# Reordering the first stages of a two-layer streaming encoder: where the norms, the weight splits and the sums of squares stand

## The chip, the cores and the metric

The kernel runs on one core of one Trainium2 chip. The metric is the device time of one execution in microseconds (us), the median of three runs. Engines are named as the profile names them: PE is TensorE (PEld its weight loads), DVE VectorE, ACT ScalarE, POOL GpSimd, SP the engine that issues the weight transfers.

## What is computed

One step of a two-layer encoder in float32 for 1024 prompt frames and 32 sample frames of 1024 channels. Cut to what matters:

```python
# layer 0: convolution module, then SwiGLU
h = rms_norm(x, g_mix0); u = h @ w_pw1 + b_pw1          # 1024 -> 2048
g = a * sigmoid(gate)                                    # a, gate = halves of u
c = depthwise_conv(g, w_dw, width 31, causal) + b_dw     # per channel
x = x + silu(layer_norm(c)) @ w_pw2 + b_pw2
x = x + (silu(rms_norm(x) @ w_gate) * (rms_norm(x) @ w_up)) @ w_down
# layer 1: sliding-window attention with per-head norms, then SwiGLU
q, k, v = split(rms_norm(x) @ w_qkv); x = x + attention(q, k, v) @ w_o
x = x + swiglu(rms_norm(x))
```

## The kernel before

The frames are held transposed (channels on the partitions) in two halves: A is frames 0 to 511 (one PSUM bank per tile), B is frames 512 to 1055 (two banks of 272 columns). Each float32 product is made of three faster products: activations and weights are split in a high part (`hAh`, `whi`) and a rest (`hAl`, `wlo`), and a tile is high x high, rest x high and high x rest. ACT writes the high part of each weight block (`hi()`, line 857), POOL the rest (`lo()`, line 1909), SP loads the raw block. `proj` (lines 346 and 355) is one tile: for each of 8 channel blocks k it waits for `h_ready` (both parts of the activations), multiplies both with `whi`, runs a piece of other PE work (`mid`), and then multiplies the high part with `wlo`. An A tile has 24 products of 512 columns, a B tile 48 of 272.

The order of the program is written out by hand for every engine, and each engine runs its list in order. The list `SEQ1` is the first stage, the tiles of `w_pw1`: gate tiles `g` and value tiles `a` of half A for the first three channel blocks, then A and B in turns, and at its end B's tiles of blocks 0 and 1. `SEQ1` index 0 to 28 is called tile 0 to 28 below. Ahead of it lie 18 groups of transposes of x (`x_group`, line 401), eight of them before tile 0, and the products `xn` that transpose and norm half A at once (line 427: x times a diagonal of the frames' norm factors, `diag`).

- While `SEQ1` runs, DVE turns each pair of tiles into a GLU output (`glu`, lines 1469 and 1475) and does the depthwise convolution of half A (`conv`, lines 1504 to 1520) in two PSUM banks X and Y, 4 and 5; ACT makes 10 of the 31 taps' products (`taps`, line 987), and POOL adds them (line 1940). After each channel block POOL adds it to a sum over channels (`csum`, line 1962).
- When `conv` of A is done, PE makes the layer norm's mean from `csum` (line 364), DVE centres (1534), ACT squares, PE sums the eight squares in float32 (`square_mean`, line 381), ACT makes the factor (`factor`, lines 881 to 885), DVE multiplies (1542), ACT does SiLU (902) and the high part (906), DVE the rest (1406), in two buffers `nrm` that are used in turns (`sq` in the profile). Only then do the eight tiles `p2` of half A run, followed by B's last tiles, half A's next norm `ffn0A`, and the feed-forward tiles.
- PSUM: banks 0 to 3 are a ring from which `take` gives the tiles their banks, 4 to 7 a second ring (transposes, head norms) or the convolution's. A bank is handed out again when its reader has released it.
- Norms later in the program (`norm_parts`): DVE x_norm (1401), ACT high part (893), DVE rest (1406), two channel blocks at a time. Their mean (`norm_mean`) takes banks of the first ring, in the middle of a tile.

## Time and profile before

| | before |
|---|---|
| median of 3 runs | 2289.23 us (2288.8 to 2289.9) |
| the profiled execution, its own time | 2286.99 us |
| its span, first to last instruction | 2285.2 us |
| mean granted PE clock | 0.988 |
| PE busy | 2228.7 us, 98% |
| POOL, DVE, ACT busy | 1113.6, 1111.8, 1037.8 us |

The profiled execution is 2.2 us below the median; 1.8 us of it lie outside the span. PE's idle time inside the span is 2285.2 less 2228.7, 56.5 us.

### The profile page before, as it was taken

What the parts mean: (1) busy time and instruction counts of PE and PEld (TensorE: products, weight loads), DVE (VectorE), ACT (ScalarE), POOL (GpSimd) and SP (SyncE); (2) the same over time, 40 slices, a digit from 0 to 9 for tenths busy, and PEclk for the clock granted to TensorE, in tenths of its full rate; (3) what the DMA queues carried; (4) which work ended last, traced back from release to release, by engine and by line L of the source; (5) the groups of instructions that cost most, each with busy time, mean ns of one, the idle gap of its engine ahead of it and who ended that gap; (6) DMA issues with size and microseconds to landing.
All of it is one profiled execution on the core that took longest, in us unless ns stands there. A gap on an engine that the chain in (4) does not pass through costs nothing.

```text
span 2285.2 us, 34556 instructions
## 1 busy us (share of the span) xinstructions
PE 2228.7 (98%) x13954; PEld 2017.0 (88%) x13954; DVE 1111.8 (49%) x1822; ACT 1037.8 (45%) x1659; POOL 1113.6 (49%) x573
## 2 busy tenths in 40 slices
PE   8998899999999999999999999999999999999999
PEld 7797678887889799999999898888888989999999
DVE  4987668873434544445443535454554142222223
ACT  6544655533524654544552466465655332222222
POOL 3787569975446533333334544333333443443433
PEclk9999899999999999999999999999999999999999
DMA  4111123332333522222222342222222323233222
GB/s 149 47 54 57 57 65 102 97 102 83 94 100 89 104 86 79 75 74 75 75 75 84 93 99 84 83 83 78 80 84 75 92 77 99 93 102 93 84 89 90
DMA packets 313644, 194.15 MB, mean 85 GB/s; under 512 B 40374, under 2 KB 286734, under 8 KB 313486
## 3 DMA queue, kind: packets, MB, share of 16 engines
q1 hardware_dynamic: 311608, 190.83, 28.3%
q8 instruction: 112, 1.84, 0.3%
q10 hardware_dynamic: 1878, 1.11, 0.2%
q14 instruction: 46, 0.38, 0.1%
HBM read 184.39 MB, written 5.10 MB: 83 GB/s over the span
## 4 chain that ended last, share of the span: by engine, by line
PE 91%; POOL 3%; DVE 2%; ACT 2%; issue 1%; DMA 0%; ACTq 0%; DVEq 0%; POOLq 0%
PE ps L346 42%; PE ps L355 21%; PE ps L560 14%; PE ps L567 7%; PE ps L530 2%; POOL accp L1940 2%; PE ps L516 1%; PE ps L364 1%; PE ps L492 1%; PE ps L491 1%; POOL wlo L1909 1%; PE ps L381 1%; DVE x L1592 1%; POOL rs L1919 0%; DVE sq L1401 0%
## 5 line engine op out<-in xcount | busy, mean ns | idle before, releaser
L1909 POOL TENSOR_TENSOR wlo<-raw,whi 128x1024 fp32r<-128x1024 f32 x342 | 838.9, 2453 | 1095.4 <-PE ps L355 763.7
L857 ACT ACTIVATE whi<-raw 128x1024 fp32r<-128x1024 f32 x342 | 361.8, 1058 | 628.4 <-PE ps L346 366.6
L346 PE MATMUL ps<-hBh,whi 128*128 128x272 f32 x2112 | 440.7, 290 | 6.0 <-DVE x L1592 3.2
L346 PE MATMUL ps<-hBl,whi 128*128 128x272 f32 x2112 | 440.0, 290 | 0.0
L346 PE MATMUL ps<-hAh,whi 128*128 128x512 f32 x1056 | 418.7, 397 | 18.5 <-DVE hAl L1406 10.5
L346 PE MATMUL ps<-hAl,whi 128*128 128x512 f32 x1056 | 416.1, 394 | 0.0
L1592 DVE TENSOR_TENSOR x<-ps,x 128x512 f32<-128x512 f32 (+1 forms) x368 | 258.4, 705 | 244.2 <-PE ps L567 181.3
L346 PEld LDWEIGHTS ps<-hBh,whi 128*128 128x128 f32 x2112 | 334.2, 190 | 8.9 <-issue 4.9
L346 PEld LDWEIGHTS ps<-hBl,whi 128*128 128x128 f32 x2112 | 332.4, 189 | 0.0
L355 PE MATMUL ps<-hBh,wlo 128*128 128x272 f32 x2112 | 291.2, 290 | 0.0
L355 PEld LDWEIGHTS ps<-hBh,wlo 128*128 128x128 f32 x2112 | 273.7, 188 | 2.5 <-issue 1.9
L355 PE MATMUL ps<-hAh,wlo 128*128 128x512 f32 x1056 | 270.6, 399 | 2.9 <-POOL wlo L1909 2.9
L346 PEld LDWEIGHTS ps<-hAh,whi 128*128 128x128 f32 x1056 | 200.3, 190 | 68.8 <-DVE hAl L1406 11.1
L1599 DVE TENSOR_TENSOR s<-ps,s 128x512 f32<-128x512 f32 (+1 forms) x88 | 62.3, 708 | 369.3 <-PE ps L355 367.2
L355 PEld LDWEIGHTS ps<-hAh,wlo 128*128 128x128 f32 x1056 | 197.0, 190 | 46.6 <-issue 4.3
L346 PEld LDWEIGHTS ps<-hAl,whi 128*128 128x128 f32 x1056 | 200.9, 190 | 40.8
L1940 POOL TENSOR_TENSOR accp<-accp,prod 128x512 f32<-128x512 f32 (+1 forms) x144 | 199.7, 1387 | 25.2 <-ACT prod L987 12.4
L1665 DVE TENSOR_TENSOR ptl<-ps,pth 128x512 fp32r<-128x512 f32 (+1 forms) x64 | 42.1, 658 | 167.1 <-ACT pth L1088 167.1
L1508 DVE SCALAR_TENSOR_TENSOR ps<-gxB,dwc,ps 128x574 f32<-128x574 f32 x152 | 114.1, 811 | 0.0
L1088 ACT ACTIVATE pth<-ps 128x512 fp32r<-128x512 f32 (+1 forms) x64 | 36.6, 572 | 167.6 <-PE ps L516 167.6
L1508 DVE SCALAR_TENSOR_TENSOR ps<-gxA,dwc,ps 128x512 f32<-128x512 f32 x152 | 101.8, 749 | 0.0
L560 PE MATMUL ps<-act0h,whi 128*128 128x272 f32 (+1 forms) x288 | 78.6, 327 | 4.5 <-DVE x L1592 3.9
(254 smaller groups left out, 3161.7 us busy)
## 6 DMA issues: line engine op xcount, KB each, us to landing
raw<-in_w_gate_dram SPq DMA_DIRECT2D x88, 512.0 KB, 3.8
raw<-in_w_up_dram SPq DMA_DIRECT2D x88, 512.0 KB, 3.8
raw<-in_w_down_dram SPq DMA_DIRECT2D x88, 512.0 KB, 3.6
raw<-in_w_pw_dram SPq DMA_DIRECT2D x38, 512.0 KB, 4.0
raw<-in_w_qkv_dram SPq DMA_DIRECT2D x32, 256.0 KB, 3.7
raw<-in_w_o_dram SPq DMA_DIRECT2D x64, 128.0 KB, 2.9
stage<-in_x_prompt_dram SPq DMA_DIRECT2D x8, 512.0 KB, 5.7
raw<-in_w_qkv_dram SPq DMA_DIRECT2D x8, 512.0 KB, 3.7
```

Of the source, the lines that this page charges most:

```text
L346: ins = nc.tensor.matmul(o, whi[n % 2][:, P * k:P * (k + 1)], src[:, k, c0:c0 + w], start=(k == 0 and src is hi_[h]), stop=False)
L355: ins = nc.tensor.matmul(o, wlo[n % 2][:, P * k:P * (k + 1)], hi_[h][:, k, c0:c0 + w], start=False, stop=(k == KD - 1))
L530: ins = nc.tensor.matmul(ps[0:HD, 6, 0:256], v[:, slot, HD * g:HD * (g + 1)], p[:, 256 * z:256 * (z + 1)], start=(z == 0 and w == 0), stop ...
L560: ins = nc.tensor.matmul(o, whi[n % 2][:, wc], src[s + e][:, c0:c0 + w], start=(e == 0 and src is ach), stop=False)
L567: ins = nc.tensor.matmul(o, wlo[n % 2][:, wc], ach[s + e][:, c0:c0 + w], start=False, stop=(e == 1))
L857: nc.scalar.activation(whi[n % 2][:], raw[n % 2][:], ACT.Copy).then_inc(w_hi, 1)
L1508: link(nc.vector.scalar_tensor_tensor((X, Y)[q % 2], two(gx[h][:, c, t:t + w]), dwc[:, KD * t + c:KD * t + c + 1], (X, Y)[q % 2], ALU.mult ...
L1592: nc.vector.tensor_tensor(xd, pt(key), xd, ALU.add).then_inc(fr(key), 1)
L1599: nc.vector.tensor_tensor(s, pt(key), s, ALU.mult).then_inc(fr(key), 1)
L1665: nc.vector.tensor_tensor(ptl[:, 0:w], ps[:, 5, 0:w], f(pth[:, 0:w]), ALU.subtract).then_inc(pt_lo, 1)
L1909: nc.gpsimd.tensor_tensor(wlo[n % 2][:], raw[n % 2][:], f(whi[n % 2][:]), ALU.subtract).then_inc(w_lo, 1)
L1940: nc.gpsimd.tensor_tensor(accp[p % 2][:, 0:w], accp[p % 2][:, 0:w], prod[r % 2][:, 0:w], ALU.add).then_inc(padd, 1)
```

## The change

1. **Start.** PE first runs 10 idle products (`keep_busy`), after the eight groups of transposes 14 more; only the norm gains, three small transfers, are waited for early (`gains_in`); the other parameters are transposed in tile 0. The `xn` products go between tile 0's own products, two blocks ahead. ACT splits weight block 0 after its first block of `hAh`, block 1 after its fifth.
2. **Half A's convolution.** ACT makes 9 taps' products per channel block instead of 10, DVE 22 taps instead of 21. The transposes of x for half B use banks 6 and 7 only (ring 2), so that the convolution starts in 4 and 5 without them; it takes 4/5 and 6/7 in turns, and the two joining steps of a block come six steps into the next one. The five diagonals for half B are made on ACT.
3. **Layer norm of half A.** The sum over channels skips POOL's last add: PE adds the last block with a second product. `SEQ1` ends with tile 26 (`g` of B, block 0). Five B tiles lie around the norm: `a`0, then `g`1 and `g`2 before `p2`, `a`1 and `a`2 after it. POOL adds the eight squares in pairs and PE sums four; for `ffn0A` DVE adds seven of them and PE sums two.
4. **Norms in place.** The normed value goes to a buffer of its own, shared with the rest's; DVE does all x_norm steps of a group and then all rests; the first tile that reads a new norm does high x high, high x `wlo`, and last the rests (`new` in `proj`).
5. **Elsewhere.** Table loads are issued ahead of the wait in `factor`; three means take ring 1; `act_low` of a feed-forward group stands after the eighth add of `x` instead of the fourth; two sums of squares stand behind a weight split; `wo`'s mean is a third of a tile later; the last norm `ffn1B` is begun between two weight blocks of `down`.

```diff
-NP = {"A": 10, "B": 10}
+NP = {"A": 9, "B": 10}
-SEQ1 += [("g", "B", 0), ("a", "B", 0), ("g", "B", 1)]
+SEQ1 += [("g", "B", 0)]
+    for p in range(KD):
+        out += own[p][:6] + ends + own[p][6:-2]
+        ends = own[p][-2:]
-        want = 0 if s < 2 else 1 if s in (5, 6) else 6 if s < 5 else 7
+        want = (0, 0, 8, 10, 10, 2, 2)[s] if s < 7 else 8
+        RINGS = [(0, 4), (4, 4), (6, 2)]
+                new = ev and (ev, h) != ("mix0", "A") and waited.get(h, 0) < h_need(ev, KD - 1)
                 for k in range(KD):
+                    if ahead is not None:
+                        ahead(k)
+                    if new:
+                        pe.wait_ge(h_hi[h], h_need(ev, k))
+                    ins = product(whi, hi_, k, start=(k == 0))
+                    if not new:
+                        ins = product(whi, lo_, k)
+                if new:
+                    for k in range(KD):
+                        wait_h(h, ev, k)
+                        ins = product(whi, lo_, k, stop=(k == KD - 1))
-            pe.wait_ge(csummed, KD - 1)
-            mean(("lm", "A"), "A", ones_d, csum)
-            proj("B", ("a", "B", 1), "mix0", load(("a", 1)))
-            square_mean("lnA", lambda k: pe.wait_ge(sq_ready, k + 1))
+            pe.wait_ge(csummed, KD - 2)
+            nc.tensor.matmul(ps[:, b, :], ones_d[:], csum[:, 0:512], start=True, stop=False)
+            pe.wait_ge(c_ready, KD)
+            nc.tensor.matmul(ps[:, b, :], ones_d[:], gx["A"][:, ORDER["A"][-1], 0:512], start=False, stop=True
+            proj("B", ("a", "B", 0), "mix0", load(("a", 0)))
+            square_sum("lnA", range(0, KD, 2), lambda i: pe.wait_ge(sq_pairs, i + 1))
+            for c in (1, 2):
+                proj("B", ("g", "B", c), "mix0", load(("g", c)))
             for d in range(KD):
-                proj("A", ("p2", "A", d), "ln", load(("p2", d)))
-            proj("B", ("g", "B", 2), "mix0", load(("g", 2)),
+                proj("A", ("p2", "A", d), "ln", load(("p2", d)), ring=0 if d else 2)
+            for c in (1, 2):
+                proj("B", ("a", "B", c), "mix0", load(("a", c)),
+            def sum_of_squares(k):
+                nc.vector.tensor_tensor(sqx[:, 0, :], sqx[:, 0, :], sqx[:, k, :], ALU.add).then_inc(sq_sums, 1)
                 for k in range(k0, k1):
                     x_norm(ev, k, gain)
-                    if k % 2:
-                        low(ev[-1], ev[:-1], k - 1)
-                        low(ev[-1], ev[:-1], k)
+                for k in range(k0, k1):
+                    low(ev[-1], ev[:-1], k)
-                        if d == 3:
+                        if d == (3 if G in (0, NG - 1) else KD - 1):
                             act_low(l, h, G, 1)
```

On PE, before tile 0, `xn` products (`diag,stage`) stood in one block. In PE's order before:

```order
L401 MATMUL ps<-ident,stage 128x128 [waits pfree3]
L427 MATMUL ps<-diag,stage 128x128 [waits diag_ready] x4
L427 MATMUL ps<-diag,stage 128x128 [waits diag_ready,pfree0]
L427 MATMUL ps<-diag,stage 128x128 [waits diag_ready] x7
L427 MATMUL ps<-diag,stage 128x128 [waits diag_ready,pfree1]
```

And the same place after the change:

```order
L470 MATMUL ps<-ones_d,ident 128x128 x14
L479 MATMUL ps<-diag,stage 128x128 [waits diag_a,pfree1]
L479 MATMUL ps<-diag,stage 128x128 [waits diag_a] x3
L395 MATMUL ps<-hAh,whi 128x512 [waits h_readyA,w_hi]
L395 MATMUL ps<-hAl,whi 128x512
L479 MATMUL ps<-diag,stage 128x128 [waits diag_a,pfree2]
```

The `xn` products of block 3 now come behind tile 0's two products of block 0, and 14 idle products lie ahead of them.

On PE, at the end of half A's convolution (`csum,ones_d` is the mean, `sqx,ones_d` the sum of squares). Before, with lines left out between them:

```order
L364 MATMUL ps<-csum,ones_d 128x512 [waits pfree2,csummed]
...
L355 MATMUL ps<-hBh,wlo 128x272 [waits w_lo]
...
L381 MATMUL ps<-sqx,ones_d 128x512 [waits sq_ready,pfree2]
L381 MATMUL ps<-sqx,ones_d 128x512 [waits sq_ready] x7
L346 MATMUL ps<-hAh,whi 128x512 [waits h_readyA,w_hi,pfree2]
```

After the change:

```order
L532 MATMUL ps<-csum,ones_d 128x512 [waits csummed,pfree2]
L534 MATMUL ps<-gxA,ones_d 128x512 [waits c_ready]
L395 MATMUL ps<-hBh,whi 128x272 [waits w_hi,pfree0]
...
L442 MATMUL ps<-sqx,ones_d 128x512 [waits sq_pairs,pfree2]
L442 MATMUL ps<-sqx,ones_d 128x512 [waits sq_pairs] x3
...
L395 MATMUL ps<-hBh,whi 128x272 [waits w_hi,pfree2]
...
L395 MATMUL ps<-hAh,whi 128x512 [waits h_hiA,w_hi,pfree6]
L395 MATMUL ps<-hAh,whi 128x512 [waits h_hiA] x7
L395 MATMUL ps<-hAh,wlo 128x512 [waits w_lo]
```

Two B tiles now stand between the sum of squares and the first `p2` tile, and that tile waits for the high parts first.

On ACT, around tiles 3 to 5 (`s<-ps` is a sigmoid, `prod` a tap's product, `whi` a weight split). Before:

```order
L968 ACTIVATE s<-ps,col 128x512 [waits pfull2]
L932 ACT_TABLE_LOAD [waits row_sq]
L933 ACTIVATE col<-col 128x5
L936 ACTIVATE col<-col 128x5 [waits row_rs]
L987 ACTIVATE prod<-gxA,dwc 128x512 [waits padd] x3
L857 ACTIVATE whi<-raw 128x1024 [waits whi_free,w_in1]
L987 ACTIVATE prod<-gxA,dwc 128x512 [waits padd] x3
L857 ACTIVATE whi<-raw 128x1024 [waits whi_free,w_in0]
L968 ACT_TABLE_LOAD [waits pfull0]
L968 ACTIVATE s<-ps,col 128x512 [waits pfree1]
```

After the change:

```order
L1102 ACTIVATE diag<-ident,col 128x128 [waits row_rs]
L1102 ACTIVATE diag<-ident,col 128x128 x3
L1102 ACTIVATE diag<-ident,col 32x32
L1104 ACT_TABLE_LOAD
L1080 ACTIVATE prod<-gxA,dwc 128x512 [waits padd] x2
L950 ACTIVATE whi<-raw 128x1024 [waits whi_free,w_in1]
L1080 ACTIVATE prod<-gxA,dwc 128x512 [waits padd] x2
L950 ACTIVATE whi<-raw 128x1024 [waits whi_free,w_in0]
L1061 ACTIVATE s<-ps,col 128x512 [waits pfull0,pfree1]
```

The diagonals came to ACT, four instead of six products stand ahead of tile 4's sigmoid, and its table is loaded before them.

## Rows read from the trace of the kernel before

**Rows 1.** The page, part 1: busy time of each engine.

```profile
PE 2228.7 (98%) x13954; PEld 2017.0 (88%) x13954; DVE 1111.8 (49%) x1822; ACT 1037.8 (45%) x1659; POOL 1113.6 (49%) x573
```

**Rows 2.** The waits of PE, whole span: us in total, times, longest.

```profile
PE ps L346 <- DVE hAl L1406: 10.5, 6, 7.1
PE ps L364 <- POOL csum L1962: 8.9, 1, 8.9
PE ps L346 <- ACT s L968: 4.8, 1, 4.8
...
PE ps L346 <- DVE x L1592: 4.0, 2, 3.2
PE ps L560 <- DVE x L1592: 3.9, 3, 1.3
PE ps L346 <- ACT qraw L1143: 3.7, 2, 1.9
...
PE ps L355 <- POOL wlo L1909: 2.9, 1, 2.9
```

**Rows 3.** Timeline, PE and ACT, the start: start, us, what, idle before.

```profile
12.09 0.21 ACT L936 ACTIVATE col<-col 128x4 f32<-128x4 f32 x1
...
16.47 9.33 PE L427 MATMUL ps<-diag,stage 128*128 128x128 f32 x64 [1.42 <-DVE diag L1434]
...
29.38 0.26 PE L441 MATMUL ps<-ident,R 42*128 42x42 f32 x1
```

**Rows 4.** Windows: stretch, length, busy of PE, PEld, DVE, ACT, POOL, then PEclk.

```profile
18.50:20.50 2.00, 2.00 (x12) 2.00 (x11) 0.75 (x1) 0.90 (x2) 0.00 (x0) 0.50 1.04 410
22.50:25.50 3.00, 3.00 (x29) 3.00 (x28) 2.83 (x4) 2.51 (x4) 1.86 (x1) 1.00 0.04 10
65.00:68.00 3.00, 2.77 (x7) 2.20 (x8) 2.10 (x3) 1.49 (x5) 1.60 (x1) 0.50 0.04 10
241.00:248.00 7.00, 6.06 (x11) 2.83 (x11) 4.93 (x8) 5.17 (x8) 0.00 (x0) 0.50 0.00 0
```

**Rows 5.** Timeline, PE: the `wlo` parts of neighbouring tiles, two of B, two of A.

```profile
191.06 2.16 PE L355 MATMUL ps<-hBh,wlo 128*128 128x272 f32 x16
...
197.09 2.16 PE L355 MATMUL ps<-hBh,wlo 128*128 128x272 f32 x16
...
254.09 1.98 PE L355 MATMUL ps<-hAh,wlo 128*128 128x512 f32 x8
...
259.53 1.98 PE L355 MATMUL ps<-hAh,wlo 128*128 128x512 f32 x8
```

**Rows 6.** Half A's convolution: DVE and PE timeline, DVE's group, window.

```profile
45.52 1.41 DVE L1504 TENSOR_SCALAR ps<-gxA,dwc 128x512 f32<-128x512 f32 x2 [5.30 <-ACT x L958]
...
214.16 2.07 PE L364 MATMUL ps<-csum,ones_d 128*128 128x512 f32 x2 [8.88 <-POOL csum L1962]
...
L1508 DVE SCALAR_TENSOR_TENSOR ps<-gxA,dwc,ps 128x512 f32<-128x512 f32 x152 | 101.8, 749 | 0.0
...
45.50:212.93 167.43, 154.17 (x953) 140.15 (x951) 150.13 (x230) 88.70 (x125) 138.21 (x97) 0.98 0.18 51
```

**Rows 7.** Timeline, PE and ACT: the sum of squares and the layer norm behind it.

```profile
223.15 7.03 PE L381 MATMUL ps<-sqx,ones_d 128*128 128x512 f32 x16
...
230.21 1.28 ACT L881 ACT_TABLE_LOAD   x1 [7.38 <-PE ps L381]
...
236.33 0.80 ACT L902 ACTIVATE sq<-gxA,col 128x512 f32<-128x512 f32 x1
237.16 0.63 ACT L906 ACTIVATE hAh<-sq 128x512 fp32r<-128x512 f32 x1
```

**Rows 8.** Windows and timeline: half A's `p2` tiles; DVE beside POOL.

```profile
250.30:288.70 38.40, 38.40 (x172) 31.81 (x171) 30.82 (x44) 23.21 (x31) 36.48 (x22) 1.00 0.29 83
...
956.38 2.39 POOL L1909 TENSOR_TENSOR wlo<-raw,whi 128x1024 fp32r<-128x1024 f32 x1 [4.90 <-ACT whi L857]
...
956.50 2.85 DVE L1604 TENSOR_TENSOR act3l<-s,act3h 128x544 fp32r<-128x544 f32 x1
```

More of the change, by code:

```diff
@@ L68, in conv_a_steps @@
             glu += 1
[L69 removed]
+        want = (0, 0, 8, 10, 10, 2, 2)[s] if s < 7 else 8
         new = KD * NQ["A"] if s == len(SEQ1) - 1 else done + want
[L71 removed]
+        while any(p >= glu for p, _ in CONV["A"][done:new]):
+            new -= 1
         out.append((done, new))
@@ L971, in _, with taps @@
             done = {"A": 0, "B": 0}
-            def taps(h, j):
-                for i in range(done[h], products(h, j)):
+            def taps(h, n):
+                for i in range(done[h], n):
                     p, c, t, r = in_order(h, i)
@@ L1929, in _, with taps @@
             summed = {"A": 0, "B": 0}
-            def taps(h, j):
-                for i in range(done[h], products(h, j)):
+            def taps(h, n):
+                for i in range(done[h], n):
                     p, c, t, r = in_order(h, i)
```

360 lines of the change are left out of this document (216 added, 144 removed).

## The prediction, made before the changed kernel was run

> **What bounds the kernel now.** I read the page's busy times first: PE is busy 98% of the span, the other four engines under half [rows 1]. So only three things can give time: PE's idle time (56.5 us, the span less its busy time), stretches in which PE runs at its lower clock, and PE work that is dropped. The second view is PE's waits: all of them together are some 51 us, and they are few [rows 2]. The largest are 10.5 us for half A's rests `hAl`, 8.9 us for POOL's `csum`, 4.8 us for a sigmoid; then 4.0 and 3.9 us for DVE's adds to x, 3.7 us for `qraw`, 2.9 us for a `wlo`. The third view is the windows with the granted clock: it stands at 0.50, the lower level of 1.2 GHz, from the `xn` products to 20.5 us, for 3 us behind the sigmoid's wait and from 241 to 248 us behind the layer norm's wait, and at 1.00 (2.4 GHz) elsewhere; each of these stretches follows one in which PE stood still or ran thinly [rows 4]. The reader is to see that nearly everything the change can win lies in the first 320 us. My yardsticks are the tile pitches at full clock: a B tile takes 197.09 - 191.06 = 6.03 us, an A tile 259.53 - 254.09 = 5.44 us [rows 5].
>
> **Start (term a, -4 us).** The factors of half A's frames are done at 12.3 us, but the first `xn` product starts at 16.47 us, since DVE's copies and the wait for all parameters stand ahead of the diagonals [rows 3]. Then 64 passes take 9.3 us, about four of them at half clock; at full clock 29 passes take 3.0 us [rows 3, 4]. After the change the first diagonal can be there at 12.7 us; 14 idle products (28 passes) begin, by my estimate, at 10.5 us, behind the transposes, and end at 13.4 us if PE is at full clock by then. From there 64 passes at 0.10 and tile 0's 16 products at a 24th of 5.44 us each make 10.3 us, so the `whi` part ends near 24 instead of 29.3 us: -5.2. Against it stands a new wait: tile 1 now gets the bank of tile 0, whose sigmoid can only start when tile 0 has ended, about 1.0 us. What I do not see is when the three gain transfers land: not before the first block of x, not after 12.7 us. If late, PE's idle products end near 18 us and the term is nothing or +1; the other end is -6. I take -4, since they are issued first on their queue.
>
> **Tile 5 (term b, -5.3 us).** Tile 5 takes tile 4's bank and waits 4.8 us for its sigmoid, because ACT first has a product that waits for POOL, a split and a table load; behind the wait PE runs 3 us at half clock, which loses 1.5 [rows 2, 4].  Less POOL work stands ahead and the table is loaded early, but ACT now makes the diagonals: two table loads and ten small operations, some 5 us in tile 3, which has slack until the middle of tile 4. The sigmoid itself stays on the path, 1.0 us. So 4.8 + 1.5 - 1.0 = 5.3; bounds 3 and 7.
>
> **The convolution's end (term c, -1.4 us).** This is the disputed place. Two B tiles fewer lie ahead of the mean, so PE arrives at 205.3 - 12.1 - 4 - 5.3 = 183.9 us (205.3 is the mean's start less its wait [rows 6]). DVE's convolution must also be done by then. Before, DVE worked 150.1 of the 167.4 us from 45.5 to 212.9, and it began 5.3 us late, because its banks were in use [rows 6]. After, it has eight steps more (8 x 0.67 = 5.4 us), five diagonals less (3.8) and one glu less (1.0): 150.7 us of work. It can begin when the second tile is done, 9 us sooner, at 36.6. With no gap it ends at 187.3, with the gaps of before (17.3 us) at 204.6. Part of these gaps were the wait for half B's factors, which should shrink with term b, and the joins' waits for POOL, which the new order moves six steps away; the rest was want of steps in the table, 7 a tile, now 8. Eight steps and the glus take DVE 23.2 us in each four tiles, PE 22.9: it is full. I take 4 us of gaps: it ends at 191.3, and PE waits 7.4 us instead of 8.9. Bounds: 3.4 us of wait (-5.5) and 20.7 us (+11.8). The second product of the mean costs about 1 us inside this wait and saves POOL's last add behind it.
>
> **Sums of squares (term d, -8.6 us).** Eight float32 products of 512 columns take 7.0 us [rows 7], about 0.86 us each at full clock. Four and six fewer of them: 10 x 0.86. What takes their place lies beside PE: POOL's four adds under the B tile ahead, DVE's six under the `p2` tiles. The two tiles that were moved are no cost in all.
>
> **The layer norm's wait (term e, -9.7 us).** From the end of the sum of squares (230.2) to the `wlo` part of the second `p2` tile (254.1) are 23.9 us; at full speed it would be 3.63 + 5.44 = 9.1, so this place costs 14.8 us: 7.1 of wait, the rest by a tile that is paced by SiLU (0.80) and the high part (0.63) for each block, at half clock [rows 2, 4, 5, 7]. After: Ln, Exp and a table load take 3 us, eight blocks at 1.38 us and two splits 13.1 us, so the last high part comes 16.1 us behind the sum; the two B tiles and seven products last 13.7. That leaves 2.4 us of wait. I add 1.5 for DVE steps that lie beside POOL's splits (below) and 1.2 for clock. 14.8 - 5.1 = 9.7; bounds 6 and 12.5.
>
> **First feed-forward tile (term f, -1.9 us).** The waits for `hAl` other than the longest are 3.4 us, most of them here, with some clock behind them [rows 2]: 4.4 us. High x high first lets PE work under the rests, but DVE now gives all eight normed blocks first and the rests later; I leave 2.5 us.
>
> **Later places (term g, -18.5 us).** Each is a wait that the order removes [rows 2]: for `wlo` 2.9; for `qraw` (a bank that the mean of the first ring blocked) 3.7; for the adds to x behind `act_low` 3.9; for the adds to x at the last norm and one other place 4.0. Behind the wait of tile 5, 3 us at half clock lost 1.5 us [rows 4]; I set 1.5 to 2 behind the three long ones here, 5.6 in all. That is 20.1; I leave 1.6 for what comes back in other places, as the last norm's rests.
>
> **Where the trace speaks against it.** A DVE step that reads two SBUF operands can stand still beside POOL: `act3l` started at 956.50, just behind a split on POOL that ran from 956.38 to 958.77, and took 2.85 us, where DVE's steps of 512 columns take 0.67 [rows 6, 8]. The GPSIMD Engine Reference of the Trainium skill (Specifications) says that GpSimd shares its SBUF interfaces with VectorE, with contention for instructions with two SBUF inputs; by that rule the new adds of squares on DVE, and x_norm, z and rests as before, meet it, but not the convolution's steps, which read one operand from PSUM. The trace agrees: 152 such steps took 0.67 us each while POOL was busy 138 of 167 us [rows 6]. In half A's `p2` stretch DVE is busy 30.8 of 38.4 us and POOL 36.5 [rows 8]. Six adds at 0.7 make 35.0 us and fit; at 2.85 they make 47.9 and do not.
>
> **The sum.** -4.0 - 5.3 - 1.4 - 8.6 - 9.7 - 1.9 - 18.5 = -49.4. The profiled execution of before took 2287.0 us, so 2237.6; the median stood 2.2 us above it, so I predict 2238.5 us.
>
> **Rivals.**
> 1. *Forecast:* as summed, 2229 to 2247; chance 0.60.
> 2. *DVE bounds the first stage:* its gaps stay at 17 us, because it must wait for glus and joins in a list with no slack. PE waits some 13 us more for the convolution: 2252. For it: DVE has 23.2 us of work for each 22.9 us of PE. Against it: most of the old gaps came from too few steps. Chance 0.20.
> 3. *POOL blocks DVE in the `p2` stretch:* 47.9 us of work in 38.4 hold back the adds to x, whose banks come back late; some 9 us: 2247. Chance 0.10.
> 4. *The later waits only move:* term g is nothing, 2257. Each is a bank or an order, named by its releaser, which speaks against all of them moving. Chance 0.05.
> 5. *Slower:* POOL and the convolution's steps do collide when DVE has no gaps. It decides when each of the 192 steps costs 54 / 192 = 0.28 us more, 0.95 instead of 0.67 us; at 1.0 us it gives +63 - 49, 2300. The 152 steps above speak against it. Chance 0.03.
> 6. *No change:* 0.02.
>
> **How the numbers follow.** A measurement of this kernel can tell 0.2%, 4.6 us, from no change. Cases 1 to 4 are all faster: 0.95; same 0.02; slower 0.03. The range takes in case 1 whole, case 3 and case 2: 2227 to 2254. The likeliest case's own range is 2229 to 2247.
>
> **What would show it.** In the profile after: the `xn` products start near 13.5 us at full clock; a wait of about 1 us for a sigmoid at tiles 1 and 5; one wait of 4 to 12 us of PE for `gxA` (the joins of DVE, no longer POOL's `csum`); DVE above 90% busy from 75 to 190 us; 2 to 5 us for `hAh` at the first `p2` tile and its pitch 5.4 us soon after; PE's waits in all 20 to 27 us instead of 51. Wrong would be the prediction if the wait at the mean is above 15 us, if the feed-forward tiles' three waits for adds to x still stand, or if PE waits for adds to x among the `p2` tiles.

## The result and the profile after

The changed kernel takes 2255.72 us (median of 4 runs, 2254.92 to 2256.87), the kernel before 2289.02 us (median of 4, 2287.04 to 2289.9) beside it: a ratio of 0.9856, 95% interval 0.9839 to 0.9873. It is 33.3 us (1.4%) faster. The prediction said 2238.5 us, 2227 to 2254: the sign was right, the gain forecast was half again too large, and the time lies 1.7 us above the range. The profiled execution took 2255.28 us with a span of 2253.5 us, where before it was 2286.99 and 2285.2, so the ledger below is made of spans: 31.7 us.

The page of the changed kernel, part 1, answers to [rows 1]:

```profile
PE 2213.8 (98%) x13984; PEld 2012.0 (89%) x13984; DVE 1113.0 (49%) x1831; ACT 1036.1 (46%) x1659; POOL 1120.2 (50%) x568
```

PE is busy 14.9 us less and idle 39.7 us instead of 56.5. The waits of PE over the whole span, as in [rows 2] (total, times, longest):

```profile
PE ps L395 <- DVE gxB L1581: 7.5, 1, 7.5
PE ps L534 <- DVE gxA L1628: 6.2, 1, 6.2
PE ps L429 <- DVE vtl L1850: 3.5, 1, 3.5
PE ps L395 <- issue: 2.8, 2, 1.6
PE ps L395 <- ACT hAh L999: 2.7, 2, 1.8
PE ps L470 <- POOL col L2017: 2.5, 1, 2.5
PE ps L395 <- DVE gxA L1575: 2.2, 1, 2.2
PE ps L395 <- ACT s L1061: 1.6, 2, 0.8
PE ps L582 <- DVE col L1739: 1.5, 1, 1.5
```

Read it against [rows 2]: every line of before is gone, has another name or has shrunk. `hAl` (10.5) is 0.6, the sigmoid (4.8) is 1.6 in two waits, `wlo`, `qraw` and both lines of adds to x are gone. The line of 6.2 us for `gxA` is the wait at the mean that the prediction kept. Five lines were in no term: `gxB` with 7.5 us (the gated product of half B's block 1), `vtl` with 3.5 us, 1.5 us for attention scores (`L582`), and in half A's convolution 2.2 us for another gated product and 1.6 of the 2.8 us of `issue`. The 2.5 us for `col` is the start of the idle products (called dummies below), ahead of the first input. All waits together are 34 us, where the prediction wanted 20 to 27.

Windows of the changed kernel (stretch, length, busy of PE, PEld, DVE, ACT, POOL, then PEclk): the first stage, the stretch of the `p2` tiles, and the two stretches of the long wait.

```profile
90.00:192.00 102.00, 102.00 (x655) 93.95 (x654) 101.14 (x161) 49.70 (x70) 89.91 (x65) 1.00 0.17 47
...
282.60:294.00 11.40, 3.88 (x22) 3.38 (x21) 11.40 (x22) 6.16 (x10) 0.80 (x2) 0.73 0.15 44
294.00:300.00 6.00, 6.00 (x19) 4.67 (x19) 5.65 (x8) 0.00 (x0) 4.59 (x3) 0.66 0.32 90
236.00:275.00 39.00, 38.59 (x185) 32.51 (x184) 35.32 (x46) 21.17 (x28) 37.85 (x22) 1.00 0.32 95
```

The first line answers to [rows 6]: DVE is busy 99% of it, POOL 88%. In the stretch with the long wait PE does 3.9 of 11.4 us of work, and in the 6 us behind it the granted clock is 0.66, so part of them is at 1.2 GHz. Among the `p2` tiles PE does not wait; the 0.4 us that are missing in the last line stand behind them, at 274.35 us, for the last square.

The timeline of the changed kernel at four places: PE's start, DVE at both ends of half A's convolution, PE at the mean, and PE at the first feed-forward tile (start, us, idle before):

```profile
11.24 3.29 PE L470 MATMUL ps<-ones_d,ident 128*128 128x128 f32 x28
...
29.93 0.50 PE L395 MATMUL ps<-hAh,whi 128*128 128x512 f32 x1 [0.78 <-ACT s L1061]
...
38.97 0.75 DVE L1575 SCALAR_TENSOR_TENSOR gxA<-ps,col,s 128x512 f32<-128x512 f32 x1 [10.17 <-PE ps L395]
...
197.21 0.75 DVE L1623 SCALAR_TENSOR_TENSOR accp<-ps,col,accp 128x512 f32<-128x512 f32 x1 [2.15 <-POOL accp L2058]
197.99 0.69 DVE L1628 TENSOR_TENSOR gxA<-ps,accp 128x512 f32<-128x512 f32 x1
...
198.74 2.07 PE L534 MATMUL ps<-gxA,ones_d 128*128 128x512 f32 x2 [6.17 <-DVE gxA L1628]
...
292.25 3.78 PE L395 MATMUL ps<-hAh,whi 128*128 128x512 f32 x8 [7.51 <-DVE gxB L1581]
295.83 3.05 PE L395 MATMUL ps<-hAh,wlo 128*128 128x512 f32 x8
```

Each of the two groups of eight products of the first feed-forward tile takes 1.98 us at full clock [rows 5]; here they take 3.78 and 3.05 us.

**The ledger.** PE's work up to a point common to both traces is compared; the two tiles moved behind the mean are taken off at 6.03 us each.

- To the mean of the layer norm (the start, tile 5 and the convolution's end; terms a, b, c): 198.74 now, 214.16 - 12.06 = 202.10 before [rows 6]. -3.4 us; forecast -10.7.
- Sums of squares (d): 7.03 became 3.60 us [rows 7], and the second sum went from eight products to 1.95 us. -8.5 us; forecast -8.6.
- The layer norm (e): from the end of the sum at 211.09 to the `wlo` of the second `p2` tile at 235.71 are 24.62 us, less 12.06 of moved tiles 12.56, less 9.1 at full speed: it costs 3.5 us where it cost 14.8. -11.3 us; forecast -9.7.
- The first feed-forward tile (f): up to a down product of the same group (379.39 now, 397.62 before, both traces with the same 0.23 us gap ahead of it) the whole is -18.2 us, so this place gave -18.2 + 3.4 + 8.5 + 11.3 = +5.0 us; forecast -1.9.
- Everything later (g): -31.7 + 18.2 = -13.5 us; forecast -18.5.

The misses are 7.3, 0.1, -1.6, 6.9 and 5.0 us: 17.7, the difference of -49.4 and -31.7.

### The profile page after: what moved, and what is told of

The parts are those of the page before. It is cut to its first block, busy times and chain, and to the rows that moved or that the text cites. A ratio compares the mean times of both kernels' runs of the same rounds, so it can differ in the third digit from the quotient of the medians.

```text
span 2253.5 us, 34607 instructions
## 1 busy us (share of the span) xinstructions
PE 2213.8 (98%) x13984; PEld 2012.0 (89%) x13984; DVE 1113.0 (49%) x1831; ACT 1036.1 (46%) x1659; POOL 1120.2 (50%) x568
## 4 chain that ended last, share of the span: by engine, by line
PE 90%; DVE 4%; POOL 3%; issue 2%; ACT 1%; DMA 0%; SPq 0%; DVEq 0%; POOLq 0%; ACTq 0%
PE ps L395 60%; PE ps L653 15%; PE ps L660 7%; POOL accp L2058 2%; PE ps L621 2%; PE ps L607 1%; PE ps L429 1%; DVE hB L1508 1%; PE ps L582 1%; PE ps L583 1%; POOL wlo L2027 1%; DVE hBl L1513 0%; POOL rs L2037 0%; PE ps L470 0%; PE ps L462 0%
## 5 line engine op out<-in xcount | busy, mean ns | idle before, releaser
L2027 POOL TENSOR_TENSOR wlo<-raw,whi 128x1024 fp32r<-128x1024 f32 x342 | 849.4, 2484 | 1053.9 <-PE ps L395 659.2
L395 PE MATMUL ps<-hBh,whi 128*128 128x272 f32 x2112 | 434.0, 289 | 5.6 <-issue 2.8
L395 PE MATMUL ps<-hBl,whi 128*128 128x272 f32 x2112 | 433.5, 289 | 0.2
L395 PE MATMUL ps<-hAh,whi 128*128 128x512 f32 x1056 | 411.4, 394 | 12.7 <-DVE gxB L1581 7.5
L395 PE MATMUL ps<-hAl,whi 128*128 128x512 f32 x1056 | 407.6, 390 | 0.0
L2058 POOL TENSOR_TENSOR accp<-accp,prod 128x574 f32<-128x574 f32 (+1 forms) x136 | 191.6, 1409 | 30.8 <-ACT prod L1080 19.0
L1196 ACT ACTIVATE pth<-ps 128x512 fp32r<-128x512 f32 (+1 forms) x64 | 36.6, 572 | 167.1 <-PE ps L607 167.1
L1616 DVE SCALAR_TENSOR_TENSOR ps<-gxA,dwc,ps 128x512 f32<-128x512 f32 x160 | 107.3, 746 | 0.0
```

The lines of the kernel that those rows point to most:

```text
L395: ins = nc.tensor.matmul(o, wt[n % 2][:, P * k:P * (k + 1)], src[h][:, k, c0:c0 + w], start=start, stop=stop)
L1196: nc.scalar.activation(pth[:, 0:w], ps[:, 5, 0:w], ACT.Copy).then_inc(pt_hi, 1)
L1616: link(nc.vector.scalar_tensor_tensor((X, Y)[q % 2], two(gx[h][:, c, t:t + w]), dwc[:, KD * t + c:KD * t + c + 1], (X, Y)[q % 2], ALU.mult ...
L2027: nc.gpsimd.tensor_tensor(wlo[n % 2][:], raw[n % 2][:], f(whi[n % 2][:]), ALU.subtract).then_inc(w_lo, 1)
L2058: nc.gpsimd.tensor_tensor(accp[p % 2][:, 0:w], accp[p % 2][:, 0:w], prod[r % 2][:, 0:w], ALU.add).then_inc(padd, 1)
```

## Experiments

The changed kernel's 2255.7 us is the yardstick of all runs; each was timed beside the kernel before, whose median stood between 2288.1 and 2290.0 us. Ratios are to the kernel before. The diffs show the lines that carry the edit; where tables of the order move with it, the text says so.

**1. The gated product ahead of the norm.** On DVE, at the end of the `p2` tiles:

```diff
+            glu("B", 1)
             norm_parts("ffn0A", C_FFN[0], 0, KD)
-            glu("B", 1)
             glu("B", 2)
```

> The changed kernel with one edit: on VectorE the gated product of half B's block 1 stands ahead of the eight norm products of the first feed-forward layer instead of behind them and their low parts. Theory (the bank): the first feed-forward tile waited 7.5 us because the bank that it takes is read by that gated product, and the half clock behind the wait cost about 2 us more. Then the wait of 7.5 us for gxB is gone, a wait of 1 to 3 us for hAh stands there, the clock is full, and the kernel takes 8 to 10 us less than the changed kernel: 2246 to 2248 us. Rival (the norm itself): the norm's products come too late anyway, since their first one stood beside GpSimd's wlo from 279 to 281 us; the wait then only changes its name to hAh, 5 us or more of it stay, and the kernel gains 3 us or less (2253 or more).

2251.67 us (2251.27 to 2252.45), ratio 0.9835 (0.982 to 0.985): 4.0 us gained, between the two theories. Its timeline of PE, and a window behind it:

```profile
285.07 1.09 PE L395 MATMUL ps<-hAh,whi 128*128 128x512 f32 x4
286.48 2.06 PE L395 MATMUL ps<-hAh,whi 128*128 128x512 f32 x4 [0.32 <-ACT hAh L988]
288.38 2.00 PE L395 MATMUL ps<-hAh,wlo 128*128 128x512 f32 x8
...
323.19 0.50 PE L395 MATMUL ps<-hAh,whi 128*128 128x512 f32 x1 [2.09 <-ACT s L1160]
...
310.00:330.00 20.00, 17.57 (x83) 13.69 (x82) 14.29 (x19) 11.54 (x17) 19.43 (x13) 1.00 0.29 86
```

At the place itself the bank theory holds in full: the wait is 0.3 us, the clock is full, and the next tile starts at 292.15 instead of 300.57 us, 8.4 us sooner. But half of it is lost on the way to the down product of 379.39 us, which starts at 375.04, only 4.4 us sooner. The largest loss is seen near 323 us: POOL is busy 19.43 of 20 us, ACT's products for half B's convolution wait for its additions, the SiLU stands behind them in ACT's list, and PE waits 2.1 us for it. The long wait had been hiding a queue on POOL.

**2. Ten taps instead of nine on POOL in half A.** One step and one product of the tables move with it, so that the joins stand behind their sums.

```diff
-NP = {"A": 9, "B": 10}
+NP = {"A": 10, "B": 10}
-        want = (0, 0, 8, 10, 10, 2, 2)[s] if s < 7 else 8
+        want = (0, 0, 8, 10, 9, 2, 2)[s] if s < 7 else 8 if s % 3 else 7
```

> The changed kernel with 10 instead of 9 of half A's 31 taps on ScalarE and GpSimd, so 8 convolution steps fewer on VectorE (0.67 us each) and 8 additions more on GpSimd (1.35 us each). Theory (VectorE bounds the first stage): VectorE is busy 99% of 90 to 192 us, so the convolution ends about 5 us earlier (193 to 195 instead of 198.7), TensorE's wait for it at the mean of the layer norm falls from 6.2 to about 1 us, and the kernel takes 4 to 5 us less: 2250.5 to 2252 us. Rival (GpSimd is as near): VectorE waits at each join for GpSimd's sum, the end of the convolution stays within 1.5 us of 198.7, and the time is 2254 to 2258 us.

2258.63 us (2257.38 to 2260.01), ratio 0.9865 (0.9851 to 0.988): 2.9 us slower than the change, and slower than the rival's range too. The rival's mechanism shows in DVE's timeline at the last join, and in the window of the stage:

```profile
199.62 0.75 DVE L1623 SCALAR_TENSOR_TENSOR accp<-ps,col,accp 128x512 f32<-128x512 f32 x1 [4.19 <-POOL accp L2058]
...
90.00:192.00 102.00, 102.00 (x649) 94.34 (x649) 97.27 (x155) 55.55 (x79) 95.94 (x69) 0.99 0.17 48
```

DVE's joins wait 12.5 us for POOL (4.8 in the changed kernel), POOL is 94% busy, and the convolution ends at 201.1 us. PE's wait at the mean is now for POOL's `csum`, 6.8 us.

**3. The mean of `ffn1A` back in banks 0 to 3.**

```diff
                     if s == 4:
-                        norm_mean(ev, 1)
+                        norm_mean(ev, 1 if h == "A" else 0)
```

> The changed kernel with the mean of the norm ffn1A back in the ring of banks 0 to 3 (that of ffn0B stays in banks 4 to 7). Theory: this turns of the ring made the head's mean take the bank of vs, whose reader on VectorE stands behind norm products (wait of 3.5 us at 1321 us). With the edit that wait is gone, and the kernel takes 3 to 4 us less: 2252 to 2253 us. Rival: the wait that the change removed at the same place in the kernel before (some 2 us) comes back, and 1.5 us or less is left of the gain (2254 or more).

2251.55 us (2250.65 to 2252.56), ratio 0.9835 (0.9818 to 0.9851): 4.2 us gained. Between 1250 and 1360 us the only wait of PE that is left is

```profile
PE ps L395 <- ACT qraw L1251: 1.4, 1, 1.4
```

where the changed kernel has the 3.5 us for `vtl`. So the wait of before does come back (1.4 us), as the rival said, and still more is won than the waits' difference of 2.1 us; the rest has no row of its own.

**4. The norm of half B in pairs again.** Two norm products and two low parts at a time for `mix0B`, as before the change:

```diff
-                for k in range(k0, k1):
-                    x_norm(ev, k, gain)
-                for k in range(k0, k1):
-                    low(ev[-1], ev[:-1], k)
+                n = 2 if ev == "mix0B" else k1 - k0
+                for i in range(k0, k1, n):
+                    for k in range(i, i + n):
+                        x_norm(ev, k, gain)
+                    for k in range(i, i + n):
+                        low(ev[-1], ev[:-1], k)
```

> The changed kernel with the norm mix0B on VectorE in pairs again (two norm products, two low parts) instead of four and four. Theory: the burst of four norm products stood beside GpSimd's wlo and took 6.0 us instead of 3, and the tiles of half B behind it waited 1.6 and 2.2 us. But what decides this stage is VectorE's work in all up to the end of the convolution, and the pairs stand beside GpSimd's work as much: the waits of TensorE near 79 and 87 us change by up to 3 us in sum, the convolution ends within 1 us of 198.7, and the time is within 1.5 us of 2255.7. Rival (the burst itself costs): VectorE gets 3 us back, the convolution ends at 196 or before, and the kernel takes 2253 or less.

2257.28 us (2256.02 to 2257.9), ratio 0.9858 (0.9844 to 0.9873): 1.6 us slower, just outside the theory's 1.5 us and away from the rival. The wait at the mean is 6.2 us as before the edit. DVE's timeline shows why the pairs do not help; the split on POOL ran from 61.79 to 64.68:

```profile
60.59 4.67 DVE L1508 SCALAR_TENSOR_TENSOR hB<-x,col,rs 128x544 f32<-128x544 f32 x2 [0.96 <-ACT rs L1110]
...
66.63 1.48 DVE L1508 SCALAR_TENSOR_TENSOR hB<-x,col,rs 128x544 f32<-128x544 f32 x2
...
61.79 2.89 POOL L2029 TENSOR_TENSOR wlo<-raw,whi 128x1024 fp32r<-128x1024 f32 x1
```

The pair beside the split takes 4.67 us, the next one, with POOL idle beside it, 1.48. It is paid once in either order.

**5. No dummy products.**

```diff
-            keep_busy(10)
-            keep_busy(14)
```

> The changed kernel without its 24 dummy products (10 ahead of the input's transposes, 14 behind them); nothing else differs. Theory: they buy the full clock for the start. Without them a half clock stands somewhere before 30 us, the first full tile starts 1 to 4 us later than 29.9 us, and the kernel takes 1 to 3 us more (2257 to 2259 us), less than the tile's delay, since the end of half A's convolution hangs on VectorE. Rival: the transposes and products keep the clock by themselves, and the 14 dummies only hold TensorE up (the second group took 3.3 us in front of the products); then the products of x start earlier and the time is 2253 to 2256 us.

2257.2 us, in the theory's range, but with 2254.57 to 2259.72 the four runs lie 5 us apart (those of the changed kernel 2 us); ratio 0.9863 (0.9848 to 0.9877). The profiled execution is the 2254.57 one, and it shows the full clock in each window from 0 to 60 us and the first full tile 1.7 us sooner:

```profile
28.25 0.50 PE L395 MATMUL ps<-hAh,whi 128*128 128x512 f32 x1 [0.78 <-ACT s L1059]
...
195.51 0.75 DVE L1621 SCALAR_TENSOR_TENSOR accp<-ps,col,accp 128x512 f32<-128x512 f32 x1 [2.14 <-POOL accp L2056]
```

So in this execution the transposes and products held the clock without help, against the theory, and the 1.7 us reached the convolution's end (197.0 instead of 198.7). The three slower runs have no trace, but their mean granted clock is on record: 0.995 for the fastest, 0.994 (2256.36), 0.994 (2258.03) and 0.993 (2259.72). So the slower ones stood longer at the lower clock; where they did is not shown. What is settled is that the second group of dummies, not the clock, made the products start at 14.37 instead of 12.6 us.

**6. `act_low` back in its old place.**

```diff
-                        if d == (3 if G in (0, NG - 1) else KD - 1):
+                        if d == 3:
                             act_low(l, h, G, 1)
```

> The changed kernel with one part undone: in the feed-forward layers the low part of the second activation stands again behind the third of the eight additions of the last down product (before the change's place behind the seventh) in every group of tiles. Theory: TensorE's down product at its fourth place then waits for an addition late by one low part, the waits of the kernel before in those layers (3.9 us in sum) come back, and the kernel takes 3 to 4.5 us more than the changed kernel: 2259 to 2260 us. Rival: the waits that vanished did so since everything in front of them stands elsewhere in time now, and the time is within 1 us of 2255.7.

2260.84 us (2259.8 to 2261.48), ratio 0.9873 (0.9859 to 0.9888): 5.1 us slower, a little over the theory's range. The other 1.3 us have no row of their own; the wait is the one of [rows 2], to 0.1 us:

```profile
PE ps L653 <- DVE x L1707: 3.8, 3, 1.3
```

**7. Edits 1 and 3 together** (the diffs are those).

> The changed kernel with both edits that each gave 4 us: half B's block 1 ahead of the first feed-forward norm, and the mean of ffn1A back in banks 0 to 3. Theory: they are a thousand microseconds apart and add up: 2247 to 2248.5 us. In the first of the two the gain of 8.4 us at the second tile (292.15 instead of 300.57) shrank to 4 since GpSimd was busy 19.4 of 20 us behind it, and that stays so here: a wait of about 2 us near 323 us. Rival: the gain is that of one alone (2251 or more).

2247.53 us (2246.07 to 2248.02), ratio 0.9819 (0.9805 to 0.9834). They add up; the wait near 323 us is again 2.1 us, and this time the granted clock of 310 to 330 us is 0.91 where it was 1.00 in run 1.

**8. Nine taps for half B too**, on top of 7, with DVE's steps at 6 instead of 5 in two more slots of a group.

```diff
-NP = {"A": 9, "B": 10}
+NP = {"A": 9, "B": 9}
-    + [((G, b), 6 if b == 4 else 5) for G in range(NG) for b in range(5) if G or b < 4]):
+    + [((G, b), 6 if b % 2 or b == 4 else 5) for G in range(NG) for b in range(5) if G or b < 4]):
```

> As the run with both edits, and in addition half B's convolution with 9 instead of 10 taps on ScalarE and GpSimd (8 steps more on VectorE, 8 additions of 1.5 us fewer on GpSimd), with VectorE's steps spread over the same slots. Theory: behind the first feed-forward tile GpSimd is what is late (7.1 of 10, 9.9 of 10 and 19.4 of 20 us busy between 290 and 330, ScalarE's products and the silu behind them waiting for its additions), so with less work on GpSimd the wait of 2 us near 323 us goes and 2 to 4 us more are gained: 2243.5 to 2246 us. Rival: VectorE, with 8 steps more, is late in its place (PE waits for adds or gated products of 1 us and more between 300 and 480 us), and the time is 2247 us or more.

2245.26 us (2244.71 to 2245.36), ratio 0.981 (0.9795 to 0.9825): 2.3 us more. The wait for the SiLU is 1.2 us instead of 2.1, and the third group of down products starts at 400.73 us instead of 403.26, so the gain is all made there, where POOL's queue stood. This supports POOL's queue as the cause of the loss in 1; DVE has more work here, not less, so it was not DVE.

**9. Less work on DVE in half A.** The first product of each running sum is made by ACT in the same bank. DVE leaves these steps out and waits for ACT's products instead; its other steps are spread a little denser, and ACT's products for POOL a little earlier:

```diff
+    for q in range(2):
+        t = NP[h] + q
+        nc.scalar.activation(ps[:, 4 + q + 2 * (n % 2), 0:512], gx[h][:, c, t:t + 512], ACT.Copy,
+                             scale=dwc[:, KD * t + c:KD * t + c + 1]).then_inc(first_two, 1)
```

> The changed kernel with one job moved off VectorE in half A's convolution: the first product of each of the two running sums (16 instructions of 0.7 us) is computed by ScalarE into the same banks; the steps are spread a little denser. GpSimd has the same work. Theory (both VectorE and GpSimd are near their limit, VectorE first): VectorE's busy time in the stage falls by 11 us, the convolution ends 3 to 6 us earlier (193 to 196 us), TensorE's wait at the mean falls by as much, and the kernel takes 3 to 5 us less: 2250.5 to 2253 us. Rival (with 9 taps GpSimd bounds it already): VectorE waits for GpSimd's sums instead, the convolution ends within 1.5 us of 198.7 and the time is 2254.5 or more.

2257.78 us (2257.08 to 2258.78), ratio 0.9867 (0.985 to 0.9883): 2.1 us slower, as the rival said. DVE's work falls (94.8 of 102 us), the end does not come sooner: DVE waits 9.0 us for ACT's products and 10.1 for POOL, the last join among them:

```profile
198.67 0.75 DVE L1647 SCALAR_TENSOR_TENSOR accp<-ps,col,accp 128x512 f32<-128x512 f32 x1 [3.49 <-POOL accp L2082]
```

**10. Four dummies behind the transposes instead of fourteen**, on top of 8.

```diff
-            keep_busy(14)
+            keep_busy(4)
```

> As the run with nine taps for half B (2245.3 us), with 4 instead of 14 dummy products behind the input's transposes; the 10 ahead of them stay. Theory: the second group holds TensorE up by 1.7 us beyond the time at which the diagonals are ready, that delay reaches the first gated product and the end of half A's convolution, and all of it is gained while the first 10 still keep the clock: 2243 to 2244 us, with a spread of the runs under 1 us. Rival: the second group is what keeps the full clock in some executions (the runs without any of them spread from 2254.6 to 2259.7), and the median is 2245.5 or more with a spread of 2 us and more.

2244.94 us (2243.28 to 2246.26), ratio 0.9804 (0.9789 to 0.9819). The convolution ends 1.9 us sooner than in 8, but the median moves by 0.3 us and the runs lie 3 us apart. The mean granted clock splits them: 0.998 for the runs of 2243.28 and 2243.9 us, 0.996 for those of 2245.99 and 2246.26. In 8 all four runs have 0.998. So the start is gained, and lost again in half of the executions by clock; which of the dummies keep it is undecided.

**11. Eight taps for half B**, on top of 8.

```diff
-NP = {"A": 9, "B": 9}
+NP = {"A": 9, "B": 8}
```

> As the run with nine taps for half B (2245.3 us), with eight: 8 more steps on VectorE, 8 additions fewer on GpSimd. Theory: the gain of the first step of this kind (2.3 us) came from GpSimd's queue between 290 and 330 us; GpSimd is still 19.6 of 20 us busy there, so another 0.5 to 1.5 us are to be had: 2243.8 to 2244.8 us. Rival: VectorE (9.99 of 10 us busy between 290 and 300, 16.9 of 20 behind) is now as late as GpSimd was, and the time is 2245.3 or more.

2242.46 us (2242.28 to 2244.32), ratio 0.9795 (0.9781 to 0.981): 2.8 us more than 8, above the theory's range; 2.1 us of it stand by the third group of down products (398.68 instead of 400.73 us). The window that lost 2.4 us of PE in 1 is now full, with DVE at 93%:

```profile
310.00:330.00 20.00, 20.00 (x97) 16.10 (x96) 18.60 (x23) 12.78 (x18) 19.71 (x11) 1.00 0.36 109
```

**12. Eight squares on PE.** The layer norm's squares are summed by eight products again, POOL's four additions are out (their lines are not shown).

```diff
-            square_sum("lnA", range(0, KD, 2), lambda i: pe.wait_ge(sq_pairs, i + 1))
+            square_sum("lnA", range(KD), lambda i: pe.wait_ge(sq_ready, i + 1))
```

> The changed kernel with one part undone: the eight squares of half A's layer norm are summed by eight products on TensorE again, without GpSimd's four additions. Theory: the mean of the squares is a link of the chain from the end of the convolution to the first tile behind the norm, so the 3.4 us of TensorE's added products count in full, though TensorE waits for hAh behind them (2.7 us in all): the waits for hAh stay as they are, and the kernel takes 3 to 3.5 us more: 2258.7 to 2259.2 us. Rival: the added products run inside those waits, and with GpSimd's 5 us of additions gone the chain starts earlier; the time is then 2256.7 or less.

2261.09 us, with 2257.07 to 2265.19 the widest of all runs; ratio 0.9881 (0.9864 to 0.9897). That is 5.4 us slower than the change, more than the theory's 3 to 3.5. At the place the theory holds: the waits for `hAh` behind the norm are unchanged, and the product of the first `p2` tile that waits first starts 3.6 us later than at 225.79,

```profile
229.43 0.49 PE L395 MATMUL ps<-hAh,whi 128*128 128x512 f32 x1 [0.87 <-ACT hAh L999]
```

The spread of 8 us has no row, since only the fastest of the four runs has a trace (mean granted clock 0.996; the others have 0.994 to 0.995). What runs 5, 10 and 12 show together is that runs of one kernel that lie some us apart differ in clock too.

**What sets the end of half A's convolution** was still open: more work on POOL (2) and less on DVE (9) had both ended it later. Three more runs.

**13. Both relieved:** eight taps in half A, and ACT makes the first products of blocks 1 to 6 only, one slot ahead. The products themselves are made as in 9; the tables of steps and products move with the taps.

```diff
-NP = {"A": 9, "B": 10}
+NP = {"A": 8, "B": 10}
+ON_ACT = range(1, 7)
+    while (n in ON_ACT and CONV[h].index((n, 2)) < CONV_A[s + 1][1]
+           and ("a", h, ORDER[h][n]) in SEQ1[:s]):
```

> The changed kernel with both engines of half A's convolution relieved: 8 instead of 9 taps on ScalarE and GpSimd (8 additions of 1.35 us fewer on GpSimd, 8 steps of 0.67 us more on VectorE), and the first product of both running sums of blocks 1 to 6 on ScalarE (12 instructions of 0.7 us fewer on VectorE), issued a slot ahead. Theory (the end hangs on both engines, so that relieving either alone moved the bound to the other): VectorE 3 us less, GpSimd 11 us less, the convolution ends 3 to 5 us earlier than 198.7, and the kernel takes 3 to 5 us less than the changed kernel: 2250.5 to 2253 us. Rival (VectorE's waits for ScalarE's products, or the place in the order where the last block's gated product stands, set the end whatever the work): the end stays within 1.5 us of 198.7 and the time is 2254.2 or more.

**15. Eight taps alone**, the counterpart of 2: `NP` of half A is 8, with the same tables of steps and products as in 13, and nothing is moved to ACT.

> The changed kernel with 8 instead of 9 of half A's taps on ScalarE and GpSimd, nothing moved to ScalarE: the counterpart of the run with ten. Theory (both are near their limit): VectorE has 5.4 us more, its joins no longer wait for GpSimd's sums, the convolution ends 1 to 4 us later than 198.7 and the time is 2256.5 to 2260 us. Rival (GpSimd alone sets the end): the convolution ends 1.5 us or more earlier and the time is 2254 or less.

13 takes 2250.39 us (2248.93 to 2253.27), ratio 0.9833 (0.9818 to 0.9848); 15 takes 2258.79 us (2258.39 to 2259.57), ratio 0.9869 (0.9853 to 0.9885). DVE's last join and the window of the stage, first of 13, then of 15:

```profile
193.86 0.75 DVE L1650 SCALAR_TENSOR_TENSOR accp<-ps,col,accp 128x512 f32<-128x512 f32 x1
...
90.00:192.00 102.00, 102.00 (x657) 94.34 (x657) 99.99 (x160) 50.56 (x72) 82.58 (x59) 1.00 0.17 48
```

```profile
198.31 0.75 DVE L1623 SCALAR_TENSOR_TENSOR accp<-ps,col,accp 128x512 f32<-128x512 f32 x1
...
90.00:192.00 102.00, 100.97 (x641) 93.09 (x640) 101.13 (x160) 45.04 (x63) 77.79 (x56) 0.99 0.17 47
```

With eight taps alone no join at the end waits for POOL, DVE stays 99% busy, and the convolution ends at 199.8 us, 1.1 us later than in the changed kernel though it began 0.6 us sooner. With both relieved it ends at 195.3, 3.3 us sooner than 198.7, though it began 0.3 us later, and PE's wait at the mean falls from 6.2 to 2.0 us. The start of the stage moves from run to run, so its length says more: from the first gated product to the end it is 159.7 to 159.8 us in the changed kernel and in runs 5, 8 and 10, which leave it as it is; 162.5 in 2, 161.0 in 9, 161.5 in 15, and 156.1 in 13 and in 14. The end hangs on both engines; nine taps had only balanced them. Two things stay open. No run takes work off POOL without giving it to DVE, and 9 and 13 differ in more than the taps: in 9 ACT's products come late, in 13 they are issued a slot ahead. What of the 156.1 is order and what is work is not separated.

**14. All that helped:** 11 and 13, with their diffs.

> The run with eight taps for half B (2242.5 us) and the relieved convolution of half A together. Theory: independent places, the gains add up: 2237.5 to 2240 us. Rival: what the end of the convolution gives comes back as a wait behind it: 2241.5 or more.

2240.05 us (2237.56 to 2240.66), ratio 0.9784 (0.977 to 0.9799): 49.0 us faster than the kernel before and 15.7 faster than the change, the best version, just above the range of its theory. The convolution's gain reaches the time in part only: 2.4 us on top of 11. The stage is 3.6 us shorter, PE's wait at the mean 3.4 us instead of 6.2.

## Why the prediction was right and wrong

**What held.** That the gain would come from few waits in the first 320 us and from dropped PE work. Term d is right to 0.1 us, and run 12 shows one half of it by itself (3.6 us at the place). Term e came out 1.6 us better: the waits for `hAh` are 0.9 and 1.8 us, and the pitch behind them is 5.44 us at once. The wait at the mean is for `gxA`, as forecast; that its length, 6.2 us, is near the 7.4 of the forecast is luck, since PE reached it at 192.6 instead of 183.9 us and DVE's end came 7.4 us late as well. The three waits for adds behind `act_low` went, and run 6 brings them back at 3.8 us, the 3.9 of the forecast. PE waits for nothing among the `p2` tiles: rival 3 is out. Its added squares do meet POOL, all six of them: they took 1.22 to 1.59 us instead of 0.7, 8.5 us in all, but DVE has room, 35.3 of 39 us. None of the three signs by which the prediction said it would be wrong came up, though its time was missed.

**Term a gave 0.6 us instead of 4, term b what it said, and neither was worth anything by itself.** The first step that failed in a is "begin, by my estimate, at 10.5 us ... and end at 13.4": they began at 11.24 and ended at 14.53, and the products, whose diagonals were ready from 12.6 us on, stood behind them. The second is the 10.3 us from there to the end of tile 0's `whi` part: they were 12.0 (14.37 to 26.34), 0.6 of it a wait for `hAl`. Tile 1 started 1.6 us sooner instead of 4.0. In tile 1 itself the transposes of x, now in two banks only, take 3.0 us instead of 2.1, with 0.45 us of waits for ACT's copies, and tile 4's `wlo` part comes 0.6 us sooner than before. Run 5 gives 1.7 us back by dropping the dummies. For b the wait is 0.8 us at full clock (forecast 1.0), and tile 5's `wlo` part is 6.0 us sooner, so b gave 5.4 of its 5.3 us (before, then after):

```profile
70.43 1.98 PE L355 MATMUL ps<-hAh,wlo 128*128 128x512 f32 x8
```

```profile
64.39 1.98 PE L395 MATMUL ps<-hAh,wlo 128*128 128x512 f32 x8
```

**Term c failed, and it carried a and b with it.** Its mechanism stood in the text (PE waits for DVE's convolution), but the end came at 198.7 instead of 191.3 us. By the step's own sum: the convolution's first step came at 39.76 instead of 36.6 (+3.2), DVE's work from there was 151.0 instead of 150.7 us (+0.3), and "I take 4 us of gaps" was 8.0 (+4.0). Two of the gaps are joins that wait for POOL, 4.8 us. The step looked at DVE alone: it counted 23.2 us of DVE work for 22.9 of PE and gave POOL no such line, though POOL was busy 138 of 167 us. Runs 2, 9, 15 and 13 show what stands in its place: the end hangs on both. A tap more on POOL ends it 2.4 us later with POOL last, a tap fewer 1.1 us later with DVE last, less on DVE alone 1.5 us later with POOL last and ACT's products late, and of these four only less on both ends it sooner. Since PE waits for this end anyway, what a and b saved ahead of it could only enlarge the wait, and did not even do that: two tiles near 79 and 87 us gave 3.8 us back (1.6 for `issue`, 2.2 for `gxA`, whose gated product stands on DVE behind half B's norm and ten convolution steps), and at 189.55 us PE was only 1.5 us ahead of before. Rival 2 had the mechanism, but its size (17 us of gaps, 2252) was too large.

**Term f failed in its mechanism.** "High x high first lets PE work under the rests" is true, and run 1 shows such a tile (0.3 us of wait). The step did not follow the bank. The tile takes a bank of half B's last `a` tiles, and the change put both of these directly ahead of it and their gated products behind all of the norm's 16 instructions in DVE's list. The forecast named DVE's new order in the norm, but not what was queued behind it: 7.5 us of wait and 2.9 us of half clock. Removed (run 1), the place is worth 8.4 us, of which 4.0 reach the end until POOL is relieved too (runs 8 and 11: 5.1 us more, by work moved from POOL to DVE in half B's convolution).

**Term g: the single waits vanished as listed, but "I leave 1.6 for what comes back" was too little.** Three came in their stead: 3.5 us for `vtl`, 1.5 us for scores, 1.8 us at the last norm. The first is by the same ring as the gain at `qraw`: the mean moved to banks 4 to 7 turned the ring by one, and the head's mean now takes the bank of `vs`, whose reader stands behind norm products. Run 3 puts the mean back in half B's `qkv` tiles and gains 4.2 of the missing 5.0 us. The other two were not tried.

**The range.** Three of the ledger's five lines missed to the same side by 5 to 7 us, two of them (the convolution and the first feed-forward tile) for one reason: a wait removed here was held against the list of before, and not against what the other engines would do in the time that it freed. The range took in one such rival at a time. The last step of the sum was loose as well: 2237.6 and the 2.2 us by which the median stood above the profiled execution make 2239.8, not 2238.5; 2239.8 would still lie 15.9 us below the measured time.

## What to carry to other kernels

When two stages or tiles trade places, follow each bank (or buffer) that the moved tile takes to its last reader, and read what stands ahead of that reader in its engine's list now. Where two helpers share a job and the split has been tuned, write one line of work for each; here each change on one side alone handed the bound to the other, and a gain showed only when both were relieved. And a long wait hides queues on other engines: when it goes, look at who was catching up in it (here POOL, 19.4 of 20 us) before booking its whole length.

## What the runs showed of the hardware

**How large a stall beside GpSimd is.** All norm products of half B in the changed kernel, by duration (minimum, median, maximum in ns), and of half A:

```profile
L1508 DVE SCALAR_TENSOR_TENSOR hB<-x,col,rs x32: 768/774/2924, 61.3 to 1841.9; 128x544 f32<-128x544 f32 x32
L1508 DVE SCALAR_TENSOR_TENSOR hA<-x,col,rs x24: 734/737/2787, 279.0 to 1343.5; 128x512 f32<-128x512 f32 x24
```

Most take 0.77 us; the longest takes 2.92 us, 2.15 us more, and a split on POOL takes 2.48 us on average. The GPSIMD Engine Reference of the Trainium skill (Specifications) speaks of contention with VectorE for instructions with two SBUF inputs. The rows here agree, and give its form: it is a standstill of up to the length of one POOL instruction: in run 4 the pair that was under way when the split began took 3.2 us more than the next, which ran with POOL idle. The added squares show where it ends. All six, then one of them with the split on POOL that was under way when it began:

```profile
L1688 DVE TENSOR_TENSOR sqx<-sqx x6: 1216/1401/1587, 242.0 to 271.9; 128x512 f32<-128x512 f32 x6
...
246.16 2.42 POOL L2027 TENSOR_TENSOR wlo<-raw,whi 128x1024 fp32r<-128x1024 f32 x1
...
247.54 1.58 DVE L1688 TENSOR_TENSOR sqx<-sqx 128x512 f32<-128x512 f32 x1
```

The split ends at 248.58 us, the add at 249.12, 0.54 us behind it. For the two others that began during a split (at 242.00 and 253.33) it is 0.54 and 0.56 us: the add does its work when the split is over, not beside it. The convolution's steps, with one operand in PSUM, are not touched: from 90 to 192 us they follow each other at 0.67 us (75.6 us for 112 of them in run 2, 80.0 for 119 in run 15) with POOL 94% and 76% busy beside them.

**Half clock behind a wait.** Ahead of the wait of 7.5 us PE had worked without a gap. After it PEclk is 0.66 over the next 6 us, and the first sixteen products of the tile took 2.9 us more than at full clock. Behind a wait of 0.3 us at the same place (run 1) the clock is full. Behind the wait of 2.1 us near 323 us it is 1.00 from 310 to 330 us in run 1 and 0.91 in run 7: the same wait cost clock in one execution and not in the other.
